# The product-key expert layer of a two-block transformer kernel: both expert tables streamed whole, in place of gathered rows

## What is computed

```python
q = (xt @ w_query).reshape(T, 8, 2, 128)
s = einsum('thpd,hpkd->thpk', q, subkeys)           # 8 heads, 2 halves, 128 sub-keys
sv, si = top_k(s, 16)
cand    = sv[:, :, 0, :, None] + sv[:, :, 1, None, :]            # 16 x 16
cand_id = si[:, :, 0, :, None] * 128 + si[:, :, 1, None, :]
top_s, pos = top_k(cand, 16);  expert = take(cand_id, pos);  gate = softmax(top_s)
act = gelu(einsum('thkd,td->thk', u_tab[expert], x))             # exact gelu
out = einsum('thk,thkd->td', gate * act, v_tab[expert])
```

## Time and profile before

| | |
|---|---|
| median of 3 runs | 1512.95 us (1512.3 to 1513.54) |
| span of the profiled execution | 1512.7 us |
| PE busy | 1384.3 us (92%) |
| DVE busy | 788.9 us (52%) |
| ACT, POOL busy | 284.5, 325.9 us |
| HBM traffic | 549 MB read, 364 GB/s over the span |
| software queue (the gathers) | 272.17 MB |
| line 4, by engine | PE 62%, DMA 32%, issue 3% |

### The profile page before, as it was taken

One profiled execution on the slowest core, in us unless ns is written; L12 is line 12 of the kernel. 1 busy time (PEld: TensorE's weight loads), 2 busy tenths in 40 slices (PEclk: granted clock), 3 DMA queues, 4 the chain that ended last, 5 costly groups with the idle time before them and its releaser, 6 DMA issues.

```text
span 1512.7 us, 16972 instructions
## 1 busy us (share of the span) xinstructions
PE 1384.3 (92%) x6354; PEld 721.6 (48%) x6354; DVE 788.9 (52%) x1912; ACT 284.5 (19%) x700; POOL 325.9 (22%) x315
## 2 busy tenths in 40 slices
PE   6999999999999999998999999997997877788787
PEld 4886665444444444443565755544453332333332
DVE  2257565232332332232534787757676666767555
ACT  1432313000000000000334433221212121212112
POOL 0001303000000000000000245444444443444451
PEclk9999999999999999999999999999999999998999
DMA  9743669999999999999343599999999999999997
GB/s 380 299 163 113 238 279 365 425 426 426 426 426 427 426 427 427 423 427 425 146 155 124 211 395 391 420 421 422 421 421 421 421 421 422 422 421 422 421 422 313
DMA packets 64579, 551.35 MB, mean 364 GB/s; under 512 B 9168, under 2 KB 9440, under 8 KB 11760
## 3 DMA queue, kind: packets, MB, share of 16 engines
q1 hardware_dynamic: 26080, 278.06, 44.5%
q0 software_dynamic: 38416, 272.17, 43.7%
HBM read 549.16 MB, written 1.05 MB: 364 GB/s over the span
## 4 chain that ended last, share of the span: by engine, by line
PE 62%; DMA 32%; issue 3%; DVE 1%; POOL 1%; ACT 1%; SPq 0%; POOLq 0%; DVEq 0%
DMA ring<-peer_uv_d,work 16%; PE ps L2051 12%; PE ps L1957 11%; PE ps L1299 7%; PE ps L2093 6%; DMA work<-peer_uv_d,work 5%; PE ps L1785 4%; DMA ring<-expert_w_d 4%; PE ps L1293 4%; PE ps L1746 3%; PE ps L2062 3%; PE ps L1614 2%; DMA consts_sb<-peer_uv_d,work 2%; DMA work<-expert_w_d 2%; DMA ring<-w_ada_d 2%
## 5 line engine op out<-in xcount | busy, mean ns | idle before, releaser
L1957 PE MATMUL ps<-ring,work 128*128 128x512 f32 x686 | 335.8, 631 | 73.0 <-ACT work L1230 71.8
L3281 DVE CUSTOM_DVE_ANT_0 ring<-ring,work 128x1024 f32<-128x1024 f32 x172 | 211.6, 1231 | 137.6 <-DMA ring<-peer_uv_d,work 136.3
L1957 PEld LDWEIGHTS ps<-ring,work 128*128 128x128 f32 x686 | 133.5, 201 | 253.7 <-issue 149.7
L2244 POOL DMA_INDIRECT ring<-peer_uv_d,work x170 | 187.9, 1105 | 231.3 <-PE ps L1957 206.5
L2051 PE MATMUL ps<-ring,work 128*64 128x512 f32 x768 | 168.1, 592 | 3.0 <-DMA ring<-expert_w_d 2.4
L1230 ACT ACTIVATE work<-consts_sb,work 128x128 f32<-128x128 f32 x256 | 85.2, 392 | 283.1 <-DVE work L3290 276.0
L1299 PE MATMUL ps<-ring,hT 128*128 128x512 f32 (+1 forms) x272 | 112.6, 569 | 1.8 <-DVE hT L3106 1.6
L2051 PEld LDWEIGHTS ps<-ring,work 128*64 128x64 f32 x768 | 57.0, 137 | 111.0 <-issue 111.0
L2824 DVE TENSOR_TENSOR work<-work,ps 128x512 f32<-128x512 f32 x16 | 11.0, 688 | 185.7 <-PE ps L2051 185.7
L2219 POOL DMA_DIRECT2D mod<-subkeys_d x1 | 0.5, 546 | 457.1 <-DVEq L2889 457.1
L1078 ACT ACTIVATE work<-ps 128x512 f32<-128x512 f32 x16 | 9.6, 597 | 430.6 <-PE ps L2051 430.6
(11 more groups left out here) (481 smaller groups left out, 1722.9 us busy)
## 6 DMA issues: line engine op xcount, KB each, us to landing
ring<-expert_w_d SPq DMA_DIRECT2D x72, 2048.0 KB, 19.3
work<-expert_w_d SPq DMA_DIRECT2D x36, 1024.0 KB, 18.6
ring<-w_ada_d SPq DMA_DIRECT2D x12, 2048.0 KB, 8.7
ring<-w_in_d SPq DMA_DIRECT2D x11, 2048.0 KB, 22.8
consts_sb<-expert_w_d SPq DMA_DIRECT2D x12, 1024.0 KB, 19.6
ring<-w_out_d SPq DMA_DIRECT2D x4, 2048.0 KB, 8.3
ring<-peer_w_query_d SPq DMA_DIRECT2D x4, 2048.0 KB, 7.7
ring<-w_in_d SPq DMA_DIRECT2D x4, 1024.0 KB, 29.8
```

Of the source, the lines that this page charges most:

```text
L1957: last = pe.matmul(ps[V_BANK[t] + n][:, :], diag[:, i % 4, :], v_row(i)[:, n * 512:(n + 1) * 512], start=(i % (16 * PH) == 0), stop=(i == ...
L2244: pool.indirect_dma_start(out=uv_rows(i), out_offset=None, in_=io["peer_uv"], in_offset=bass.IndirectOffsetOnAxis(ap=idx[:, s, k:k + 1], a ...
L3281: dve.tensor_tensor_reduce(out=u_row(i), in0=u_row(i), in1=h_tok[:, i // (16 * PH), :], scale=1.0, scalar=0.0, op0=ALU.mult, op1=ALU.add, ...
```

## The change

The two tables are handed over as separate arrays, reordered by the second sub-key number: block e holds the 128 experts whose second number is e, for u with features on the partitions, for v with experts on the partitions. Nothing is gathered any more.

1. **SP** streams 128 blocks of u, then 128 of v (512 KB each) through 6 places.
2. **u stage**, 64 steps of two blocks. PE multiplies each block by the normed features of all 256 tokens (8 products of 256 columns a block, `dots`), ACT writes gelu of the 128 x 256 result into `weight`, which fills all of `ring` and half of `work` at the end: 128 blocks x 256 tokens. Every expert's product is computed for every token.
3. **Routing** loses parts 20 to 24; all groups run back to back on DVE, and the softmax is done once per tile (`gates_of`). The results are turned over on PE (`picks_turned_over`) so that picks stand on partitions.
4. **Gates**, 32 sets of 8 tokens, one set per step from step 30 to 61: DVE writes two one-hot matrices of 128 x 8 x 128 (`hot_rows`), POOL multiplies the first by the gates, PE multiplies them token by token (8 products of 128 columns, `gate_rows_of`), which gives for each token the gates of all 16384 experts. DVE multiplies the part of `weight` that is ready by them (`gated_rows`), ACT copies the rest into `weight` (`kept_gates`), where later gelus are multiplied in (`late_rows`).
5. **v stage**: for each block 2 x 2 products of 512 columns, `weight` by v, into four banks; the last 6 blocks are taken bank by bank so that three of the sums are added and written out early.
6. The queries are no longer interleaved with picks; both tiles' normed features (`scaled_features`, DVE, 1024 elements each) must stand before the u stage starts. `query_norm` goes.

```diff
+N_STEPS = N_BLOCKS // 2
+SET = 8
+N_SETS = T // SET
+STEP0 = 30
+EXP_STEP = (8, 28)
+TURN_STEP = (12, 33)
+TABLE_PLACES = 6
+DOT_BANKS = 3
+def gated_at(step):
+    return SET * max(0, min(N_SETS, step + 2 - STEP0))
+weight = arena[:, 0:N_BLOCKS * T].rearrange("p (e n) -> p e n", n=T)
+by_token = arena[:, 0:N_BLOCKS * T].rearrange("p (e n) -> p n e", n=T)
 # SP
-            sp.dma_start(nw[:, :], io["norm2_w"].to_broadcast([P, D])).then_inc(in_nw4, 16)
+            sp.wait_ge(b2, BLK2.done("q00"))
+            for i in range(2 * N_BLOCKS):
...
+                if i == 5:
+                    sp.wait_ge(hn_ready, 2)
+                reused = i - TABLE_PLACES
+                if 0 <= reused < N_BLOCKS:
+                    sp.wait_ge(dots_done, reused + 1)
+                elif reused >= N_BLOCKS:
+                    sp.wait_ge(v_done, reused - N_BLOCKS + 1)
+                sp.dma_start(table_places[i % TABLE_PLACES], table[e, :, :]).then_inc(...)
 # ACT: exp_gates, applied (gelu, diag) go
+            def kept_gates(j):
+                for i in range(2):
+                    g = 2 * j + i
+                    first = 2 * (STEP0 + j - 1)
+                    act.wait_ge(gated, g + 1)
+                    act.activation(by_token[:, 4 * g:4 * g + 4, first:], b4(ps[OUT_BANK + g % 4])[:, :, first:], ACT.Copy)
+            for p in range(N_STEPS):
...
+                if STEP0 <= p < STEP0 + N_SETS:
+                    kept_gates(p - STEP0)
+                act.wait_ge(dots_done, 2 * p + 2)
+                if n < T:
+                    act.activation(weight[:, 2 * p:2 * p + 2, n:], b[:, :, n:], ACT.Gelu)
+                if n:
...
+                    act.activation(late[p % 2][:, :, 0:n], b[:, :, 0:n], ACT.Gelu)
 # PE: values goes
+                def dots(p):
...
+                    for i in range(2):
+                        wt = expert_table(2 * p + i).rearrange("p (k n) -> p k n", n=PK)
+                        for k in range(KC):
+                            last = pe.matmul(ps[p % DOT_BANKS][:, i * T:(i + 1) * T], wt[:, k, :], hn[:, k, :], ...)
+                for t, g in LATE_QUERIES:
+                    query(t, g)
+                    key_scores(*before)
+                    before = (t, g)
+                key_scores(*before)
+                row_of_scales(1)
+                pe.wait_ge(hn_ready, 2)
+                for p in range(N_STEPS):
...
+                    if STEP0 <= p < STEP0 + N_SETS:
+                        gate_rows_of(p - STEP0)
+                    dots(p)
+                v_sums()
 # POOL: the 256 gathers go
+            for j in range(N_SETS):
+                t, at = j * SET // P, j * SET % P
+                pool.wait_ge(hot_ready, j + 1)
+                pool.tensor_tensor(hot0[j % 2], hot0[j % 2], picked[t][:, 2, at:at + SET].unsqueeze(2).to_broadcast(...), ALU.mult)
 # DVE
+            def hot_rows(j):
+                dve.wait_ge(picked_ready, t + 1)
+                if j >= 2:
+                    dve.wait_ge(gate_rows, 2 * (j - 2) + 2)
+                dve.tensor_tensor(hot0[j % 2], numbers, of(0), ALU.is_equal).then_inc(hot_ready, 1)
+                dve.tensor_tensor(hot1[j % 2], numbers, of(1), ALU.is_equal).then_inc(hot_told, 1)
+            def gated_rows(j):
+                first = 2 * (STEP0 + j - 1)
+                for g in (2 * j, 2 * j + 1):
+                    dve.wait_ge(gate_rows, g + 1)
+                    dve.wait_ge(gelu_done, gelus(STEP0 + j - 2))
+                    rows = by_token[:, 4 * g:4 * g + 4, 0:first]
+                    dve.tensor_tensor(rows, rows, b4(ps[OUT_BANK + g % 4])[:, :, 0:first], ALU.mult)
+            def late_rows(p):
+                n = gated_at(p)
+                dve.wait_ge(gelu_done, gelus(p))
+                dve.wait_ge(gates_kept, n // 4)
+                dve.wait_ge(gated, n // 4)
+                rows = weight[:, 2 * p:2 * p + 2, 0:n]
+                dve.tensor_tensor(rows, rows, late[p % 2][:, :, 0:n], ALU.mult)
+            scaled_features(0)
+            for r in range(1, NG):
+                routes(r, 0, PARTS)
+                if r == 1:
+                    scaled_features(1)
+            gates_of(0)
+            for r in range(NG, N_ROUTE):
+                routes(r, 0, PARTS)
+            gates_of(1)
+            hot_rows(0)
+            for j in range(N_SETS):
+                if j + 1 < N_SETS:
+                    hot_rows(j + 1)
+                gated_rows(j)
+                late_rows(STEP0 + j - 1)
+            for p in range(STEP0 + N_SETS - 1, N_STEPS):
+                late_rows(p)
```

More of the change, by code:

```diff
@@ L42 @@
 PH, PK, PTOP = 8, 128, 16
-BATCH = 4
 RING = 6
@@ L303, with gelus @@
             apart=(("ggt1", 6), ("q00", 7)))
[L304 to L344, removed]
+N_BLOCKS = PK
+N_STEPS = N_BLOCKS // 2
[6 more added lines that the diff above has]
+DOT_BANKS = 3
+TURN_BANK = 3
+OUT_BANK = 4
+LAST_BLOCKS = 6
+def gated_at(step):
+    return SET * max(0, min(N_SETS, step + 2 - STEP0))
+GELU_OPS = [1 + (0 < gated_at(p) < T) for p in range(N_STEPS)]
+def gelus(p):
+    return sum(GELU_OPS[:p + 1])
 B2_LAST = ("pq1", "pk1", "gqk1", "pv1", "gvv1", "ggt1")
@@ L1255, in _, with exp_gates @@
-            applied(at, 16 * N_STEP)
+            query(0, 1)
+            features_in("xT", 1, cols2)
+            query(0, 2)
+            key_scores(0, 1)
+            root(5)
+            before = (0, 2)
+            for t, g in LATE_QUERIES:
+                query(t, g)
+                key_scores(*before)
+                before = (t, g)
+            key_scores(*before)
+            def exp_gates(t):
+                act.wait_ge(e_in, t + 1)
+                tile = gates[:, NG * t:NG * t + NG, :, :]
+                act.activation(tile, tile, ACT.Exp).then_inc(e_act, 1)
@@ new lines, in gate_rows_of @@
+                def gate_rows_of(j):
+                    pe.wait_ge(hot_told, j + 1)
+                    pe.wait_ge(hot_weighted, j + 1)
+                    for i in range(2):
+                        g = 2 * j + i
+                        if g >= 4:
+                            pe.wait_ge(gates_kept, g - 3)
+                        else:
+                            bank_empty(OUT_BANK + g)
+                        for c in range(4):
+                            last = pe.matmul(ps[OUT_BANK + g % 4][:, c * P:(c + 1) * P], hot0[j % 2][:, 4 * i + c, :],
+                                             hot1[j % 2][:, 4 * i + c, :], start=True, stop=True)
+                        last.then_inc(gate_rows, 1)
@@ L3293, in result @@
[L3293 to L3307 removed]
+            PARTS = 20
@@ new lines, in gates_of @@
+            def gates_of(t):
+                tile = gates[:, NG * t:NG * t + NG, :, :].rearrange("p a b c -> p (a b) c")
+                dve.wait_ge(e_act, t + 1)
+                o(dve.tensor_reduce(gsum, tile, AX.X, ALU.add))
+                sync()
+                o(dve.reciprocal(gsum, gsum))
+                sync()
+                o(dve.tensor_tensor(tile, tile, bc(gsum.unsqueeze(2), [P, PH, 16]), ALU.mult))
+                post(picks_ready)
+            numbers = bc(consts[:, C_IOTA:C_IOTA + PK].unsqueeze(1), [P, SET, PK])
@@ L3321, in _ @@
             gla_state(2)
-            routes(0, 8, 22, 0)
+            routes(0, 8, PARTS, 0)
             moba_out(1)
```

402 lines of the change are left out of this document (160 added, 242 removed).

## The result

The changed kernel takes 1871.48 us (median of 4 runs, 1870.74 to 1872.04); the kernel before took 1513.06 us beside it. The ratio is 1.237, with a 95% interval of 1.2354 to 1.2389: slower by 358 us, where 1403 us and faster were forecast. The profiled execution has a span of 1869.0 us.

The account below looks back on a forecast made before the run. The prediction took transfers to bound the kernel before. After it: first set's POOL product done at 1008.7, 31 x 5.15 = 159.7 us of sets, last gates 0.9, steps 10.4, v stage 219.7, tail 3.7: 1403 us, range 1374 to 1432.

Parts of the forecast that it names:

- late queries: Before the u stage: five late queries with scores, 3.57 + 0.45 us each, bringing PE to 901.1 us.
- start of the u stage: The u stage starts at 903.7 us, after PE's last scores at 902.3 and `scaled_features(1)` at 903.6.
- tail: After the last product: one add and one write, 3.7 us, as before.
- What bounds the kernel before: Expert layer of the old kernel: it goes at the pace of the gathers, 637.6 us at 421 GB/s.
- Transfers: Streamed table blocks: 1.24 us a block, a lone block landing in about 4.0 us; transfers leave the path.
- PE's products: Table products on PE: u step 3.455 us, gate products 0.89 us a step, v stage 219.7 us.
- Routing: DVE's routing beside the u stage: 15.8 us a group, at most 18.9, hidden by 2 to 3 us only.
- The gate stage: Steps 30 to 61: 5.15 us a set from DVE and POOL taking turns, against PE's 4.35.
- A: Gate stage: POOL and DVE don't hold each other up, PE sets the pace, 1378 us; 0.20 with partly cheaper cases.
- B: Gate stage: strided products cost double, 3.54 ns an element, 5.9 us a set, 1426 us; chance 0.14.
- C: Gate stage: slower than before through the 1 KB stride, needing 8.7 us a set; chance 0.05.
- D: Table stream: half-megabyte blocks don't keep up, showing only under 303 GB/s; 1430 us at 280 GB/s; chance 0.06.

Follow-up runs that it names:

- one-pass run of it: The kernel before, with PE reading only the upper 16 bits of weights and v rows: 1510.29 us, ratio 0.998.
- one-pass kernels: The changed kernel with u, gate and v products reading only the upper 16 bits of every number: 1361.59 us, ratio 0.8997.
- the kernel in which PE had room: The changed kernel with half of the u and v products left out and gate products reading only the upper 16 bits: 1421.16 us.
- the kernel with four tokens side by side: The changed kernel with all table products on upper 16 bits, gated rows and kept gates walked block by block, four neighbouring tokens together: 1345.03 us.

## Why the prediction was wrong

It failed at one step, in four terms. **"A run of 32 products of 256 columns took 6.91 us: 0.216 us each"**: it was 16 products, 0.432 us each. The same division is in the gate products (0.1116 for 0.223), in the v stage (0.429 for 0.858) and in the late queries (3.57 for 7.15 us each). From the forecast's own sum to the profiled span, by the chain above (us; the first and the last row are points in time, the others lengths):

| | forecast | measured | difference |
|---|---|---|---|
| start of the u stage | 903.7 | 926.1 | +22.4 |
| from there to the first gate products | 105.0 | 207.8 | +102.8 |
| 31 sets | 159.7 | 269.8 | +110.1 |
| last gates and steps | 11.3 | 22.5 | +11.2 |
| v stage | 219.7 | 439.5 | +219.8 |
| tail | 3.7 | 3.3 | -0.4 |
| end | 1403.1 | 1869.0 | +465.9 |

Point by point:

- *What bounds the kernel before*: right. The gathers, shown by the one-pass run of it, 0.998.
- *Transfers*: right in kind. They left the path; the median landing of a block was 3.6 to 3.7 us for 4.0 forecast. In the one-pass kernels, where they come back onto it, a block takes 1.28 us for the 1.24 I took.
- *PE's products*: wrong by exactly 2, as above. With half the products the kernel ends at 1421.2, inside the range that the prediction gave (1374 to 1432), so what was wrong beside this step was small in sum. Its profiled span, 1418.9, is 22.6 us over the forecast by the first gate products (1031.3 for 1008.7, the late queries again), 7.6 us under it in the 31 sets, and within 2 us in every other part.
- *Start of the u stage*: the five late queries of 7.15 for 3.57 us, with scores of 0.89 for 0.45, make 20 of the 22.4 us, and the five query parts ahead of them (8.9 for 4.5 us) 4.5 more, of which 2.5 are taken back by the projections, which ended at 872.7 for 875.2; the copies and `scaled_features(1)` (1.23 us at 924.81) stood where the forecast had them.
- *Routing*: 15.9 us a group (985.0 to 1000.9) for 15.8. It was done at 1048.7, 73.7 us before DVE got the exponential of the second tile, and so hidden with a wide margin, and not with 2 to 3 us, since PE needed 6.91 us a step. In the one-pass kernel it was not hidden: 23.0 us of waiting.
- *The gate stage*: 8.69 us, all PE's: 1.78 + 6.91. In the kernel in which PE had room, a set took 4.90 us on average, for 5.15 forecast. That the size is near is partly luck, for the mechanism was another: POOL's product takes turns with DVE's two-operand instructions, but fell beside the gated rows, whose second operand is in PSUM, and shortening it gave only 3.5 us in all. What makes 4.90 is DVE's own chain, forecast at 4.6: the gated rows cost 2.29 ns an element and not 1.77. Only in the kernel with four tokens side by side, where the gated rows take half as long, does POOL's product set the pace as forecast, at 4.29 us a set. In the changed kernel the gated rows are 58.9 us in 32 sets, 1.84 us a set for 1.4:

```profile
L3329 DVE TENSOR_TENSOR arena<-arena,ps 128x232 f32<-128x232 f32 (+31 forms) x64 | 58.9, 943 | 119.4 <-PE ps L1989 118.8
```

- *The rivals*: A had PE as the bound, with its work still halved. B and C priced the right instruction, and its price lay between the forecast's 1.77 and B's 3.54; C, the only rival on the slower side, needed 7.6 and didn't come: the kernel is slower for another reason than C's. D was not met. None of them priced a product at other than the earlier trace rows divided by its count, though 335 of the forecast's 499 us after 903.7 (30 steps, the last steps, the v stage) hung on it.

Two things would have caught it. One is the count of all records of L1957, 1020 for 510 products. The other is arithmetic on the forecast's own numbers: 512 columns in 0.429 us at 2.4 GHz are 2.0 cycles a column, a figure that I took without asking what it was made of. The Trainium skill (FP8 and Floating Point Precision, "TensorE Precision Notes") says that true float32 takes 4 passes through the array; the trace agrees, with 0.858 us for 512 columns against about 0.23 in bfloat16. An estimate from that page's 4 passes, 4 x 512 columns at the upper clock of 2.4 GHz, is 0.853 us.

## What to carry to other kernels

Divide a run of products by the number that the code issues, and hold that number against the count of the records before any price is built on it; where they differ, the price of one is the whole run over the code's number. A change that trades transfers for products has to be priced on the data type first: here the same streaming is 24% slower with float32 products, 6% slower with v alone in one pass, and 10% faster with all of the tables' products in one pass (11% with the turned walk). When a chain of vector instructions sets the pace, the walk through SBUF is worth a look: turning two axes, so that four neighbours lie together in 16 bytes, nearly halved an instruction. Once it is shorter, look again at what it had hidden: here POOL's product.

## What the runs showed of the hardware

- A float32 product is two records in the trace, each with a weight load; 512, 256 and 128 columns take 0.858, 0.432 and 0.223 us of the path, so the time goes by columns and not by loads. A bfloat16 product is one record.
- A DVE product that reads and writes SBUF with a stride of 1 KB costs 2.29 ns an element; with four elements together and 1 KB from group to group 1.08, as without a stride (480 elements: 1222, 651 and 651 ns); PSUM read with a stride of 512 bytes added nothing.
- DVE with two SBUF operands and POOL wait for each other in either order, and the wait stands in the record as part of the instruction's length: 2.81 for 1.22 us on DVE behind POOL's product, 1.21 us for 64 elements on POOL behind DVE's comparison. A DVE instruction with its second operand in PSUM isn't held up: 2.27 and 2.28 us for two gated rows of 464 elements with and without POOL beside them.
- In the kernel before with its products in one pass, the granted clock fell to 0.57, near the lower of the two levels (1.2 GHz), over a stretch in which PE was busy for 52.2 of 150 us, and the kernel's time fell by 0.2% only, with the transfers' share at 1.01 as before.
